# The adaLN modulation units: sums over partitions by two fp32r matmuls with ones in place of four single-column fp32 matmuls, and four units moved from TensorE to VectorE

## The reference

```python
mod_x = jnp.einsum('bd,lde->lbe', jax.nn.silu(c), w_ada) + b_ada[:, None, :]
mod_c = jnp.einsum('d,lde->le', jax.nn.silu(c_ctx), w_ada) + b_ada
for i in range(DEPTH):
    sh1, sc1, g1, sh2, sc2, g2 = jnp.split(mod_x[i][:, None, :], 6, axis=-1)
    csh1, csc1, cg1, csh2, csc2, cg2 = jnp.split(mod_c[i][None, None, :], 6, axis=-1)
    hx = rmsnorm(x, norm_mix[i]) * (1.0 + sc1) + sh1
    hc = rmsnorm(ctx, norm_mix[i]) * (1.0 + csc1) + csh1
    ...   # GLA (i = 0) or SWA (i = 1), residual x + g1 * mixer
    ...   # norm with sc2, sh2, SwiGLU, residual x + g2 * ffn
```

## Time and profile before

| | |
|---|---|
| time, 3 runs | 1684.82, 1686.62 (median), 1689.59 us |
| profiled execution | 1690.2 us, span 1688.5 us |
| busy share of the span | PE 97%, DVE 52%, ACT 35%, POOL 6% |
| mean granted TensorE clock | 0.988 of 2.4 GHz |
| HBM read | 149.71 MB, 90 GB/s over the span |

### The profile page before, as it was taken

How to read it: one execution, slowest core, us unless ns; L and a number is a source line. 1 busy time by engine, 2 the same in 40 slices (tenths; PEclk the granted TensorE clock), 3 DMA queues, 4 the chain that set the end, 5 groups by cost and what they waited for, 6 DMA issues and landing times.

```text
span 1688.5 us, 24409 instructions
## 1 busy us (share of the span) xinstructions
PE 1639.7 (97%) x9600; PEld 1374.5 (81%) x9600; DVE 870.1 (52%) x1458; ACT 583.3 (35%) x865; POOL 104.1 (6%) x95
## 2 busy tenths in 40 slices
PE   7999999999999999999999999889999999999998
PEld 5789988888888888888888888666768788888886
DVE  5414436545675565665655346677755633333334
ACT  5324457443331211211102234457743422222123
POOL 0000000000000000000000000045540000000003
PEclk8999999999999999999999999989999999999999
DMA  9332300013434433433343122420002232333322
GB/s 336 95 125 70 106 26 26 26 50 118 127 106 124 125 113 111 125 114 113 121 125 117 51 69 75 112 63 1 1 2 87 80 87 95 100 99 100 100 87 88
DMA packets 197312, 156.08 MB, mean 92 GB/s; under 512 B 6691, under 2 KB 194255, under 8 KB 197231
## 3 DMA queue, kind: packets, MB, share of 16 engines
q1 hardware_dynamic: 197230, 154.97, 30.0%
HBM read 149.71 MB, written 2.10 MB: 90 GB/s over the span
## 4 chain that ended last, share of the span: by engine, by line
PE 86%; DVE 5%; ACT 4%; DMA 2%; SPq 1%; issue 1%; DVEq 0%; ACTq 0%
PE ps L560 83%; PE ps L1095 2%; DVE w_lo L1642 1%; ACT w_hi L1168 1%; DMA w_raw<-in_ffn_w_in 1%; DMA ada_pre<-in_w_ada 1%; SPq L360 1%; DVE q_st L2167 1%; DVE h_lo L1705 1%; DVE scaled L1696 0%; ACT h_hi L1218 0%; DMA q_sw<-q_rot 0%; PE ps L875 0%; DVE q_rot L2118 0%; SPq L479 0%
## 5 line engine op out<-in xcount | busy, mean ns | idle before, releaser
L560 PE MATMUL ps<-h_hi,w_hi 128*128 128x256 f32 (+1 forms) x1392 | 421.8, 361 | 9.4 <-DVE w_lo L1642 8.3
L560 PE MATMUL ps<-h_hi,w_lo 128*128 128x256 f32 (+1 forms) x1392 | 413.5, 355 | 0.0
L560 PE MATMUL ps<-h_lo,w_hi 128*128 128x256 f32 (+1 forms) x1392 | 409.9, 353 | 0.0
L1642 DVE TENSOR_TENSOR w_lo<-w_raw,w_hi 128x2048 fp32r<-128x2048 f32 (+1 forms) x88 | 197.1, 2240 | 215.3 <-ACT w_hi L1168 215.2
L560 PEld LDWEIGHTS ps<-h_hi,w_hi 128*128 128x128 f32 x1392 | 257.1, 189 | 55.3 <-issue 15.6
L1168 ACT ACTIVATE w_hi<-w_raw 128x2048 fp32r<-128x2048 f32 (+1 forms) x88 | 165.1, 1876 | 386.5 <-DMA w_raw<-in_ffn_w_in 210.6
L560 PEld LDWEIGHTS ps<-h_lo,w_hi 128*128 128x128 f32 x1392 | 263.2, 189 | 38.0
L560 PEld LDWEIGHTS ps<-h_hi,w_lo 128*128 128x128 f32 x1392 | 262.7, 189 | 37.2
L560 PE MATMUL ps<-a_hi,w_hi 128*128 128x512 f32 (+1 forms) x528 | 160.4, 358 | 0.1
L560 PE MATMUL ps<-a_hi,w_lo 128*128 128x512 f32 (+1 forms) x528 | 160.1, 358 | 0.0
L560 PE MATMUL ps<-a_lo,w_hi 128*128 128x512 f32 (+1 forms) x528 | 158.0, 354 | 0.0
(11 more groups left out here) (247 smaller groups left out, 2036.0 us busy)
## 6 DMA issues: line engine op xcount, KB each, us to landing
w_raw<-in_ffn_w_in SPq DMA_DIRECT2D x88, 512.0 KB, 4.9
ada_w<-in_w_ada SPq DMA_DIRECT2D x41, 1024.0 KB, 5.2
w_raw<-in_ffn_w_out SPq DMA_DIRECT2D x32, 512.0 KB, 4.1
w_raw<-in_gla_w_in SPq DMA_DIRECT2D x24, 512.0 KB, 4.9
ada_pre<-in_w_ada SPq DMA_DIRECT2D x7, 1024.0 KB, 11.1
w_raw<-in_ffn_w_out SPq DMA_DIRECT2D x16, 384.0 KB, 3.4
w_raw<-in_gla_w_o SPq DMA_DIRECT2D x8, 512.0 KB, 7.3
w_raw<-in_swa_w_o SPq DMA_DIRECT2D x8, 512.0 KB, 4.5
```

The lines of the kernel that those rows point to most:

```text
L560: return pe.matmul(o, w, r, start=start, stop=stop, skip_group_check=skip)
L1642: dve.tensor_tensor(w_lo[s][:, 0:kc, :], raw_of(n)[:, 0:kc, :], w_hi[s][:, 0:kc, :].bitcast(F32), ALU.subtract).then_inc(wlo_ok, 1)
```

## The change

The partition sum of a DVE-made unit is now two fp32r matmuls into PSUM bank 7: an array of ones (128 x 128, `ones_r`) is the weight and `u_acc` (2 x 256 columns), split into `u_hi` and `u_lo`, streams past it. Every partition of the bank then holds all 512 sums; DVE multiplies the bank with the identity, repeated four times, so that each partition keeps its own, and reduces 4 x 128 to 4 (`store_sum`). ACT makes `u_hi` (`unit_high`), DVE `u_lo` (`unit_low`). Units 0 to 3, beside the q and k slabs, are made this way instead of on PE. Units 12 and 13 are too, and no longer beside slabs 16 and 17: units 12 to 39 are moved two slabs on, to slabs 18 to 45. Units 4 to 11 stay on PE. There are two sets of `u_acc`, `u_lo`, `u_hi` and `ones_r`, as other buffers lie in their places at different times. In the first v slab the gate projection moves from behind two token tiles to behind three.

```diff
     def has_unit(n):
-        return n < R0 or GO0 <= n < N_UNITS + R_SLOTS
+        return n < R0 or GO0 <= n < F0 or F0 + 2 <= n < N_UNITS + R_SLOTS + 2
     def unit_of(n):
-        return n if n < R0 else n - R_SLOTS
-
-    U0 = F0 + 2 - R_SLOTS
+        return n if n < R0 else n - R_SLOTS if n < F0 else n - R_SLOTS - 2
+
+    U1 = F0 - R_SLOTS
...
+        load_unit(1)
         load_slab(3, 0, cols(gla_w_in[0], 768))
-        load_unit(1)
         load_unit(2)
...
         def unit_sum(a, i=0):
             pe.wait_ge(mod_ok, a + 1 + i)
-            pe.wait_ge(ada_done, a + 1 + i)
-            for e in range(2):
-                for m in range(2):
-                    last = mm(bank(6, 2 * e + m, 1), u_acc[:, m, e * P:(e + 1) * P], ones[:, 0:1], True, True)
+            pe.wait_ge(ul_ok, sum_no(a) + 1 + i)
+            for j, u in enumerate((u_hi, u_lo)):
+                last = mm(bank(7), ones_r[u_set(a)][:, :], u[u_set(a)][:, :, :].rearrange("p m n -> p (m n)"), j == 0, j == 1)
             last.then_inc(turned, 1)
...
-        unit(0)
-        slab(QK0 + 2, 0, h_in, BOTH, turns=0, before={5: lambda: unit(1), 7: lambda: unit_turn(1)})
-        unit(2)
-        slab(QK0 + 3, 0, h_in, BOTH, turns=2)
-        unit(3)
+        pe.wait_ge(or_ok, 1)
+        slab(QK0 + 2, 0, h_in, BOTH, before={1: lambda: unit_sum(0), 7: lambda: unit_sum(1)})
+        slab(QK0 + 3, 0, h_in, BOTH, before={6: lambda: unit_sum(2)})
         pe.wait_ge(gwl_ok, 1)
-        pe.wait_ge(row_ok, V0)
+        pe.wait_ge(mod_ok, V0)
...
-                if t == 1:
-                    if n == V0:
-                        pe.wait_ge(gl_ok, 1)
+                if t == 1 and n > V0:
                     unit_turn(n - 1)
-                if t == 2:
+                if t == 2 and n == V0:
+                    pe.wait_ge(gl_ok, 1)
+                    unit_sum(n - 1)
+                if t == 2 + int(n == V0):
                     pe.wait_ge(mod_ok, n + 1)
                     gate_pre((n - V0) // 2, (n - V0) % 2)
...
-                    first_slab(n, 2 * l, segs, turn=unit_of(n) - 1 if has_unit(n) else None)
-                    a = unit_of(F0)
-                    slab(n + 1, 0, h_in, segs, k_wait=h_wait(2 * l + 1, per),
-                         before={1: lambda: unit_turn(a), 4: lambda: unit(a + 1), 7: lambda: unit_turn(a + 1)}
-                         if has_unit(n) else {})
+                    first_slab(n, 2 * l, segs, turn=U1 - 1 if l == 0 else None)
+                    slab(n + 1, 0, h_in, segs, k_wait=h_wait(2 * l + 1, per))
...
+        def unit_high(a, i=0):
+            act.wait_ge(ada_done, a + 1 + i)
+            act.wait_ge(turned, a + 1 + i)
+            if a == 0:
+                act.wait_ge(wlo_ok, QK0 + 3)
+            act.activation(u_hi[u_set(a)][:, :, :], u_acc[u_set(a)][:, :, :], ACT.Copy).then_inc(row_ok, 1)
...
+        def unit_low(a, i=0):
+            dve.wait_ge(row_ok, a + 1 + i)
+            dve.tensor_tensor(u_lo[u_set(a)][:, :, :], u_acc[u_set(a)][:, :, :], u_hi[u_set(a)][:, :, :].bitcast(F32),
+                              ALU.subtract).then_inc(ul_ok, 1)
+
+        def store_sum(a, i=0):
+            dve.wait_ge(turned, a + 2 + i)
+            part = u_acc[u_set(a)][:, :, :].rearrange("p m (e n) -> p (m e) n", n=P)
+            dve.tensor_tensor(part, bank(7).rearrange("p (c n) -> p c n", n=P),
+                              ident[:, :].rearrange("p (o n) -> p o n", o=1).to_broadcast([P, 4, P]), ALU.mult)\
+               .then_inc(up_ok, 1)
+            dve.wait_ge(up_ok, 2 * sum_no(a) + 1 + i * 2)
+            dve.tensor_reduce(den[:, :], part, AX.X, ALU.add).then_inc(up_ok, 1)
+            dve.wait_ge(up_ok, 2 * sum_no(a) + 2 + i * 2)
+            e = unit_cols(a) + i * 2
+            dve.tensor_tensor(mods[:, bass.ds(e, 2), :], den[:, :].rearrange("p (m e) -> p e m", m=2),
+                              v3(vec[:, bass.ds(V_BADA + e, 2)], 2), ALU.add).then_inc(mod_ok, 1)
...
                 if a_ is not None:
-                    store_unit(a_, i * 2)
+                    unit_low(a_, i * 2)
+                    store_sum(a_, i * 2)
```

More of the change, by code:

```diff
@@ L152, in trunk @@
     m_next = at("m_next", TM + 41088, [P, P], BF16)
-    u_acc = at("u_acc", TM + 37504, [P, 2, 256])
+    u_acc = [at(f"u_acc{j}", TM + o, [P, 2, 256]) for j, o in enumerate((32768, 37504))]
+    u_lo = [at(f"u_lo{j}", TM + o, [P, 2, 256], F32R) for j, o in enumerate((32768, 37504))]
+    u_hi = [at(f"u_hi{j}", TM + o, [P, 2, 256], F32R) for j, o in enumerate((8 * ROW, 33408))]
+    ones_r = [at(f"ones_r{j}", TM + o, [P, P], F32R) for j, o in enumerate((34816, 35456))]
     scaled_t = [at(f"scaled{j}", TM + (7 + j) * ROW, [P, T]) for j in range(2)]
@@ L230, in trunk @@
     bw_done, br_ok, ua_ok = sems("bw_done", "br_ok", "ua_ok")
+    ul_ok, up_ok, or_ok = sems("ul_ok", "up_ok", "or_ok")
     amul_ok, t_ok, hh_ok, h_ok = sem("amul_ok"), sem("t_ok"), sem("hh_ok"), sem("h_ok")
@@ L274, in has_unit, with sum_no, u_set @@
     def has_unit(n):
-        return n < R0 or GO0 <= n < N_UNITS + R_SLOTS
+        return n < R0 or GO0 <= n < F0 or F0 + 2 <= n < N_UNITS + R_SLOTS + 2
     def unit_of(n):
-        return n if n < R0 else n - R_SLOTS
-    U0 = F0 + 2 - R_SLOTS
+        return n if n < R0 else n - R_SLOTS if n < F0 else n - R_SLOTS - 2
+    U1 = F0 - R_SLOTS
+    def sum_no(a):
+        return a if a < V0 else a - U1 + V0
+    def u_set(a):
+        return int(a >= U1)
     def unit_cols(a):
@@ L449, in ffn @@
                 j0 = 0
-                for pairs in ((2, 2), (4,), (2, 1))[PARTS.index((f0, fc))]:
+                for pairs in ((1, 1, 1, 1), (4,), (2, 1))[PARTS.index((f0, fc))]:
                     m = n + 2 * j0
@@ L779, in first_slab @@
                     last.then_inc(bw_done, 1)
-                    if turn is not None:
-                        unit(turn + 1)
                 pe.wait_ge(rl_ok, 8 * e + k + 1)
@@ L1007, in ffn @@
                     for e in range(2):
-                        slab(m + e, i, h_in, segs, sums=unit_of(m) + e if has_unit(n) else None)
+                        slab(m + e, i, h_in, segs, sums=unit_of(m) + e if has_unit(m) else None)
                 if after:
                     for e in range(2):
-                        slab(n + fc - 2 + e, 0, h_in, segs)
+                        m = n + fc - 2 + e
+                        slab(m, 0, h_in, segs, sums=unit_of(m) if has_unit(m) else None)
                 n += fc
@@ L1291, in _ @@
         split(QK0 + 4)
+        unit_high(2)
         qk_out(QK0 + 3)
-        unit_row(3)
+        unit_high(3)
         act.wait_ge(gl_done, 1)
@@ L1448, in first, with up @@
                 act.activation(a_hi[:, 0, a:T], tmp[2 + s][:, a:T], ACT.Copy).then_inc(ah_ok, 1)
-            def up(n, i, u, fu, kc, ahead=True):
+            def up(n, i, u, fu, kc, ahead=True, a_=None):
                 if ahead:
                     split(n + 1, i, kc)
+                if a_ is not None:
+                    unit_high(a_, i * 2)
                 s = n % 2
@@ L1481, in ffn @@
                             split(n + e + 1, i)
+                            if has_unit(n):
+                                unit_high(unit_of(n) + e, i * 2)
                 else:
@@ L1855, in _ @@
         dve.memset(g_w[:, :, :], 0.0).then_inc(gw_ok, 1)
+        dve.tensor_copy(ones_r[0][:, :], ones[:, :]).then_inc(or_ok, 1)
+        unit_acc(0)
         split(QK0 + 2)
-        store_unit(0)
+        unit_low(0)
+        store_sum(0)
+        unit_acc(1)
         split(QK0 + 3)
-        store_unit(1)
-        store_unit(2)
+        unit_low(1)
+        store_sum(1)
+        unit_acc(2)
         split(QK0 + 4)
+        unit_low(2)
         dve.wait_ge(gwh_ok, 1)
@@ L1864, in _ @@
            .then_inc(gwl_ok, 1)
-        store_unit(3)
+        store_sum(2)
+        unit_acc(3)
+        unit_low(3)
+        store_sum(3)
         def logs(h, d):
@@ L2008, in plain @@
                 store_unit(unit_of(n))
+        dve.wait_ge(go_ok, 2 * GH)
+        dve.tensor_copy(ones_r[1][:, :], ones[:, :]).then_inc(or_ok, 1)
         scale_rows(32, V_NFFN)
@@ L2099, in ffn @@
                             if has_unit(n):
-                                store_unit(unit_of(n) + e, i * 2)
+                                unit_low(unit_of(n) + e, i * 2)
+                                store_sum(unit_of(n) + e, i * 2)
                             residual(n + e, i, segs, l * 48 + 40, i * 4 + 2 * e, None)
```

38 lines of the change are left out of this document (18 added, 20 removed).

## The result

The changed kernel takes 1672.17 us (median of 4 runs, 1668.8 to 1673.9), the kernel before 1686.63 (4 runs, 1684.82 to 1689.59): ratio 0.991, 95% interval 0.9889 to 0.9932. Forecast was 1670, in a range of 1658 to 1677. The profiled execution took 1671.42 us.

The account below looks back on a forecast made before the run. PE, busy 97% of the span, was taken as the bound. Terms -10.9 (sums), -5.1 (units 0 to 3), -1.1 and +0.9 (units 12 and 13) gave -16.2 us: forecast 1670 us, range 1658 to 1677.

Parts of the forecast that it names:

- The sum's price: PE, 26 sums of DVE-made units: two fp32r matmuls cost 0.46 us instead of 0.88, gaining 10.9 us.
- QK's units: Units 0 to 3 beside q and k slabs leave PE: 5.1 us gained, 0.8 given back by slower pace, DVE in time.
- Units 12 and 13: Ahead of slab 18: 3.3 us removed, a w_lo wait leaves 1.1 gained; two added sums lose 0.9.
- The turn of DVE: First feed-forward block: DVE's added steps cost 0, with 1.6 us to spare at u_lo and 1.4 before the SwiGLU product.
- Rival 4: Slabs 18 to 45: DVE's longer turn makes PE wait before chunk 7; 1692 us at 6 us of added steps; chance 0.03.
- Rival 1: First feed-forward block keeps 0.347 us a pair without fp32 blocks: 9.7 us more gained, 1661 us; chance 0.35, fully or partly.
- The sum: Whole kernel: the terms total -16.2 us, profiled span from 1688.5 to 1672.3 us, median forecast 1670.
- From slab 50 on: Stretches no edit touches: prediction counts as wrong if they move by more than a us.

Follow-up runs that it names:

- sums alone: Kernel before with only units 14 to 39 summed by the two fp32r matmuls, units 0 to 3, 12 and 13 left as they were: 1677.2 us, 0.9935.
- the halves: Changed kernel with the weight split for slab 18 (and slab 60) done in two halves on DVE and ACT: 1667.38 us, single run.
- Three picks: Changed kernel with DVE's product with the identity repeated three more times in each of slabs 18 to 45: 1672.81 us, 0.9908.
- six picks: Changed kernel with DVE's product with the identity repeated six more times in each of slabs 18 to 45: 1706.6 us, single run.
- QK's units back: Changed kernel with units 0 to 3, beside the q and k slabs, put back on PE: 1676.55 us, 0.9941.
- both edits: Changed kernel with feed-forward sums moved inside the first pair of each slab's last k, and slab 18's weight split halved: 1659.02 us, 0.9827.

## Why the prediction was right

- **The sum's price: right.** Forecast 0.46 against 0.88 us; measured 0.453 (17.413 - 16.96), and sums alone take 0.433 us a slab. By the 131 ns that the Trainium skill (TensorE: Matmul & The Clock Gate, section Back-to-back issue gap) gives for a 512-column matmul in a sustained stream of weight loads and matmuls it would, as an estimate, have been 0.26 us. The two starts in slab 20, 0.23 us apart, speak against that here.
- **QK's units: right in kind, 0.5 us short.** 5.1 us forecast, on the assumption that slabs 2 and 3 and the gate keep the slower pace. From the last pair of slab 1 to slab 4 it was 118.61 - 74.99 = 43.62 us instead of 49.27, 5.65 less. The pace was the term: PE was at the slower one only between the second and third sum, for some 40 of the 120 pairs, which costs 0.3 us and not 0.8. Slab 4 itself started 6.1 us earlier, but part of that is 0.33 us of an earlier start and 0.16 from slab 1, which ran at the faster pace this time. Undoing the edit cost 5.8 us. DVE was in time as worked out: 1.8 us to spare ahead of unit 1's sum (`u_lo` done at 88.56, taken at 90.36).
- **Units 12 and 13: right.** The shift between the two kernels' slab ends grew by 2.29 us in slabs 16 and 17 and fell by 1.15 in slab 18. The new wait for `w_lo` is there, 1.1 us and not 2, since less than 3.3 us was removed. The net of 1.14 us meets the forecast of 1.1 partly by luck. It holds the cheaper sum of slab 18, 0.43 us, which the forecast counts among the 26, and it has lost 0.3 us in each of slabs 17 and 18 by the pace, which was the faster in both before and is the slower now. The exchange of a hidden delay for a wait is what the halves then mostly removed.
- **The turn of DVE: right, and now measured.** Margins forecast 1.6 and 1.4 us; read 1.7 and 1.26. Three picks hide, six do not. Rival 4 did not come; the six picks show that it named the right place and about the right bound.
- **Rival 1, the pace: did not come, but its reason was wrong.** It held fp32 blocks to be what flips the pace. The new sums flip it too (slab 19 faster, 20 to 45 slower), slab 18 came out slower straight behind the wait for `w_lo`, and fp32 sums inside a pair leave it fast. The prediction said that nothing showed what two 512-column matmuls do to it; that was the open point. Of the 9.7 us it priced, another edit got 9.2 in slabs 18 to 49.
- **The sum.** Forecast 16.2 us; 17.4 behind slab 45. The difference is mostly 0.5 us of QK's pace, 0.5 from ahead of the first edit, which is no effect of the change that I can show, and 0.3 from slab 19's faster pace. Between the medians only 14.5 us are left, so that 1672.17 lies within 3 us of the forecast says less about the terms than the trace does.
- **From slab 50 on**, where no edit reaches, the trace gains a further 1.3 us, over the bound of 1 us that the prediction set itself. Slabs 62, 71 and 84 took 0.4 to 0.5 us longer in the trace of before and not in this; in that of the kernel with QK's units back slab 83 did, by 1.0. It is no effect of the change that I can show.

## What to carry to other kernels

When one engine is busy for 97% of the span, price an edit by the distance between starts on that engine, and check the helper's turn for its margins: extra work up to the sum of them was free here (2.2 of 3 us), and what went beyond it (4.4 us of work) was paid in every slab. A small block that is pushed into a regular stream can leave the stream in a slower rhythm long after the block itself; compare the pace behind it with the pace elsewhere, and try the block in another place too. Here moving it was worth 8 us and making it cheaper 11.

## What was not expected of the hardware

The alternation of a 256- and a 512-column matmul, each with its weight load, has two rhythms that hold themselves up for hundreds of microseconds: 0.347 and 0.353 us a pair, at the full granted clock (1.00 by the profile from 550 to 950 us in both). I read from PE's starts which of the two stood ahead of each sum of the first feed-forward block and which behind it. Left out is the kernel with six picks, where PE waits at the sum; there the faster pace came back in five slabs.

| sum | faster ahead of it | slower ahead of it |
|---|---|---|
| between two pairs, nine kernels | 8 times, slower behind it in all 8 | 240 times, still slower behind it in 238 |
| inside a pair, three kernels | 79 times, still faster behind it in all 79 | 3 times, faster behind it once |

That the place inside a pair keeps the faster pace is well founded; that it also brings it rests on one turn. And the upper row is no general law: in slabs 2 and 3 of the changed kernel the sums stand between pairs too, and the pace was faster behind the first, slower behind the second, faster behind the third. Why the place decides in the feed-forward block is not settled. Format is ruled out in both places, width between pairs.

The time of slab 12 is 22.6, 24.2 or 25.8 us from one profiled execution to the next. In each of them PE waits 1.8 us, and behind that wait comes a stretch at a granted clock of 0.50, the lower of its two levels (1.2 GHz), which can be short, long or absent. The rows of slab 12, from its start to that of slab 13 (PE busy, weight loads, DVE, ACT, POOL, granted clock, DMA), of the changed kernel, of the sums alone, and of both edits:

```profile
351.55:375.72 24.17, 22.40 (x137) 18.99 (x137) 10.19 (x13) 6.41 (x7) 0.00 (x0) 0.93 0.28 87
```

```profile
358.49:384.25 25.76, 23.99 (x137) 20.57 (x137) 10.19 (x13) 6.40 (x7) 0.00 (x0) 0.87 0.26 82
```

```profile
352.23:374.81 22.58, 20.81 (x136) 17.75 (x136) 10.18 (x13) 6.40 (x7) 0.00 (x0) 1.00 0.29 94
```

The work is the same, 136 or 137 matmuls, and DVE and ACT are busy for the same time; the granted clock is 0.93, 0.87 and 1.00. From the start of slab 53 to that of slab 55, with the attention in it, the traces differ in the same way, 184.3 to 188.2 us. This is not what sets the two main traces 18.8 us apart, for they agree in both places (24.2 us each, 187.7 and 187.8). It bears on the medians: of 25 later runs of the kernel before, the ten with a mean granted clock of 0.990 or more took 1684.4 to 1688.3 us, the others 1689.1 to 1693.8. At 0.987 the kernel before took 1689.1 to 1693.8 us and the changed kernel 1671.4 to 1673.9, 15 to 22 apart. For the runs behind the median of 1686.63 the clock is not on record, so it is likely and not shown that most had the higher one. Kernels within 3 us of each other are told apart slab by slab and not by their ends.
